# All seventeen column tiles of the side projection beside the delta-net; SiLU of every gate tile in the output stage

## The reference

```python
def rmsnorm(x, gain):
    xf = x.astype(jnp.float32)
    y = xf * lax.rsqrt(jnp.mean(xf * xf, axis=-1, keepdims=True) + RMS_EPS)
    return (y * gain.astype(jnp.float32)).astype(x.dtype)
...
    u = jnp.einsum('btd,dn->btn', rmsnorm(h, g_pre), w_in)
    sizes = (D_A, D_KV_A, D_KV_A, D_B, D_B, D_B, C_CONV, C_HEADS, C_HEADS, D_MIX)
...
def stick_breaking(q, k, v, q_pos, k_pos):
    z = jnp.einsum('bqhd,bkhd->bhqk', q, k, preferred_element_type=jnp.float32) * (HEAD_DIM ** -0.5)
    visible = k_pos[None, :] < q_pos[:, None]
    log_beta = jax.nn.log_sigmoid(z)
    log_keep = jnp.where(visible, jax.nn.log_sigmoid(-z), 0.0)
    later = lax.cumsum(log_keep, axis=3, reverse=True) - log_keep
    w = jnp.where(visible, jnp.exp(log_beta + later), 0.0)
    return jnp.einsum('bhqk,bkhd->bqhd', w.astype(v.dtype), v)
```

## Time and profile before

| | |
|---|---|
| median of 3 runs | 2087.07 us (2084.28 to 2088.69) |
| span of the profiled execution | 2087.2 us |
| PE busy | 1956.1 us, 94% of the span |
| DVE busy | 824.0 us, 39% |
| ACT busy | 759.4 us, 36% |
| POOL busy | 499.1 us, 24% |
| mean granted TensorE clock | 0.968 |
| side products (L330), of PE's time | 592.5 us in 1360 matmuls |
| HBM traffic | 51 GB/s over the span |

### The profile page before, as it was taken

One profiled execution on the slowest core, in us unless ns is written; L12 is line 12 of the kernel. 1 busy time (PEld: TensorE's weight loads), 2 busy tenths in 40 slices (PEclk: granted clock), 3 DMA queues, 4 the chain that ended last, 5 costly groups with the idle time before them and its releaser, 6 DMA issues. The chain is left out here.

```text
span 2087.2 us, 25680 instructions
## 1 busy us (share of the span) xinstructions
PE 1956.1 (94%) x9682; PEld 1222.7 (59%) x9682; DVE 824.0 (39%) x1596; ACT 759.4 (36%) x1590; POOL 499.1 (24%) x436
## 2 busy tenths in 40 slices
PE   6989993999999999999989998999999999969997
PEld 6944441666666666666645554555555555647775
DVE  5723432223222222222216775444454444553332
ACT  4413541222222222222214443344344444455564
POOL 0004312123222231223100000233332333324433
PEclk9999996999999999999998998999999999989999
DMA  4210204100000111102001112000100000165562
GB/s 127 95 32 10 65 1 27 32 27 32 21 32 27 62 57 37 32 27 67 21 28 45 41 41 73 11 21 17 61 28 11 21 7 11 39 180 155 168 191 89
DMA packets 120887, 108.13 MB, mean 52 GB/s; under 512 B 34337, under 2 KB 96065, under 8 KB 120769
## 3 DMA queue, kind: packets, MB, share of 16 engines
q1 hardware_dynamic: 117616, 95.62, 16.5%
q0 software_dynamic: 3152, 10.91, 1.4%
HBM read 65.54 MB, written 41.08 MB: 51 GB/s over the span
## 5 line engine op out<-in xcount | busy, mean ns | idle before, releaser
L330 PE MATMUL side_acc<-hT,wslot 128*128 128x512 f32 (+1 forms) x1360 | 592.5, 546 | 4.4 <-DMA wslot<-in_w_in 4.4
L1570 DVE TENSOR_TENSOR_SCAN prod<-keepb,prod 128x512 f32<-128x512 f32 (+4 forms) x184 | 208.4, 1133 | 286.8 <-ACT keepb L1509 286.4
L1552 POOL TENSOR_TENSOR beta<-beta,prod 128x512 f32<-128x512 f32 (+4 forms) x184 | 174.9, 951 | 588.0 <-DVE prod L1570 588.0
L330 PEld LDWEIGHTS side_acc<-hT,wslot 128*128 128x128 f32 x1360 | 218.3, 192 | 146.0 <-issue 135.6
L1509 ACT ACTIVATE keepb<-b_z 128x512 f32<-128x512 f32 (+4 forms) x184 | 97.7, 531 | 298.4 <-PE b_z L1443 191.2
L460 PE MATMUL acc<-hT,wslot 128*128 128x512 f32 (+1 forms) x480 | 180.6, 532 | 5.4 <-DMA wslot<-in_w_in 5.4
L1440 PE MATMUL b_z<-reg 64*128 64x512 f32 (+3 forms) x360 | 179.9, 580 | 4.8 <-PEq L1793 4.8
L724 POOL TENSOR_TENSOR atl<-at,cf 128x512 f32<-128x512 f32 x102 | 139.8, 1404 | 173.0 <-DVE at L944 173.0
L964 DVE TENSOR_TENSOR xt<-xt,b_kq 128x512 f32<-128x512 f32 x85 | 58.4, 688 | 303.5 <-PE b_kq L791 303.5
L1467 PE MATMUL b_o<-wt,vrow 128*64 128x128 f32 x1232 | 173.4, 280 | 0.5 <-DVE wt L1584 0.5
L1467 PEld LDWEIGHTS b_o<-wt,vrow 128*64 128x64 f32 x1232 | 129.5, 136 | 35.2 <-issue 33.7
(11 more groups left out here) (197 smaller groups left out, 2773.6 us busy)
## 6 DMA issues: line engine op xcount, KB each, us to landing
uT_scratch<-side_stage SPq DMA_DIRECT2D x36, 256.0 KB, 2.0
hT<-mix_scratch SPq DMA_DIRECT2D x17, 512.0 KB, 6.7
hT<-sz_scratch SPq DMA_DIRECT2D x17, 512.0 KB, 8.1
sz_scratch<-side_stage SPq DMA_DIRECT2D x32, 256.0 KB, 2.0
reg<-in_x_prompt SPq DMA_DIRECT2D x15, 512.0 KB
wslot<-in_w_in SPq DMA_DIRECT2D x15, 512.0 KB, 4.0
xres<-in_x_prompt SPq DMA_DIRECT2D x15, 512.0 KB
out_y_prompt<-yy POOLq DMA_DIRECT2D x15, 512.0 KB, 6.4
```

Of the source, the lines that this page charges most:

```text
L330: last = pe.matmul(self.acc[:, n % 2, 0:width], wslot[:, t % 2, k, :], hT[:, k, c0:c0 + width], start=(k == 0), stop=(k == KT - 1))
L1552: pool.tensor_tensor(w, w, prod[0:R, rowno[s] % 2, k0 + 1:k0 + nk + 1], ALU.mult).then_inc(w_ready, 1)
L1570: dve.tensor_tensor_scan(prod[0:R, row % 2, k0:k0 + nk][:, ::-1], kv, kv, prod[0:R, row % 2, k0 + nk:k0 + nk + 1], ALU.mult, ALU.bypass).t ...
```

## The change

`RAWZ` goes from 4 to 8, so all eight z tiles are made beside the delta-net as raw z, and `stick_breaking` gets none. `POINTS` holds 38 pieces in an iteration where it held 29 (four in all are never used: 18 x 38 = 684 for 680 pieces). In `stick_breaking` the pieces, `keep`, `gate`, the weight loads and the stores go; two tiles of its own (`kstage`, `b_kr`) take the turned keys, without the waits on the side projection; the swaps of the last two token blocks are issued at the start of the stage. In `output`, `zsig` and both SiLU instructions are twice as wide (128x1024). `SWAPS` follows from `POINTS`: units 28, 36, 50 become 28, 47, 66.

```diff
-RAWZ = 4
+RAWZ = 8
...
-                POINTS = [4, 2, 2, 2] + [2, 1, 1] + [2, 2, 1] * 3 + [0]
+                POINTS = [4, 2, 3, 2] + [3, 2, 2] + [2, 3, 2] * 2 + [2, 2, 2] + [0]
...
-                side = SideProjection(st, "silu", side_tiles)
+                kstage = sb("kstage", [P, 2, 2 * VBW], st=st)
+                b_kr = pb("b_kr", [P, 2, 512], st)
...
-                        side.transfers(sp, swap)
-
-                        sp.wait_ge(side.acc_ready, side.units)
+                        for b in range(SWAPPED, NBLK):
+                            c0, w = BLOCKS[b]
+                            sp.dma_start(mix[0:4, :, c0:c0 + w].rearrange("k p t -> p k t"), reg[:, 0:4, c0:c0 + w]).then_inc(spilled[b], 16)
+                            sp.dma_start(reg[:, KS:KS + 2, c0:c0 + w], uT[7:9, :, c0:c0 + w].rearrange("k p t -> p k t")).then_inc(qk_in[b], 16)
+                            sp.wait_ge(spilled[b], 16)
+                            sp.dma_start(reg[:, QS:QS + 2, c0:c0 + w], uT[5:7, :, c0:c0 + w].rearrange("k p t -> p k t")).then_inc(qk_in[b], 16)
...
                         for s in range(N + 4):
                             if s < N:
                                 scores(s)
-                                side.products(pe, side_piece(s), side_piece(s + 1) - side_piece(s))
...
                                 sigmoids(s)
-                                for n in side_units(s):
-                                    side.keep(act, n)
...
                                 scan(s)
-                                for n in side_units(s):
-                                    side.gate(dve, n)
```

More of the change, by code:

```diff
@@ L1293, in _, with stick_breaking @@
                         dve.tensor_copy(krow[:, :, :], b_pt[:, 0, 0:2, :]).then_inc(krow_kept, 1)
-        def stick_breaking(side_tiles):
+        def stick_breaking():
             KC = 512
@@ L1320, in stick_breaking @@
                 new = slice(SP0, SP0 + NSAMP)
[L1322 to L1327, removed]
                 steps = []
@@ L1410, in _ @@
                                 for dst, part in b_key_stores(m):
-                                    sp.dma_start(dst, side.stage[part, g % 2, (m % 2) * VBW:(m % 2 + 1) * VBW]).then_inc(krow_out[g % 2], 16)
+                                    sp.dma_start(dst, kstage[part, g % 2, (m % 2) * VBW:(m % 2 + 1) * VBW]).then_inc(krow_out[g % 2], 16)
                             for dst, src in pieces[len(pieces) * g // GROUPS:len(pieces) * (g + 1) // GROUPS]:
@@ L1471, in turn_keys @@
                         def turn_keys(g):
-                            if g < 2:
-                                pe.wait_ge(side.staged, side.units)
-                            else:
+                            if g >= 2:
                                 pe.wait_ge(krow_kept, g - 1)
@@ L1478, in turn_keys @@
                                     at = (m % 2) * VBW + a * P
-                                    last = pe.transpose(side.acc[:, g % 2, at:at + P], reg[:, KS + a, m * P:(m + 1) * P], ident)
+                                    last = pe.transpose(b_kr[:, g % 2, at:at + P], reg[:, KS + a, m * P:(m + 1) * P], ident)
                             last.then_inc(krow_turned, 1)
@@ L1519, in keep_keys @@
                             act.wait_ge(krow_turned, g + 1)
-                            if g < 2:
-                                act.wait_ge(side.stored[g], 16 * ((side.units + 1 - g) // 2))
-                            else:
+                            if g >= 2:
                                 act.wait_ge(krow_out[g % 2], krow_transfers(g % 2, g))
                             width = VBW * len(key_group(g))
-                            act.activation(side.stage[:, g % 2, 0:width], side.acc[:, g % 2, 0:width], ACT.Copy).then_inc(krow_kept, 1)
+                            act.activation(kstage[:, g % 2, 0:width], b_kr[:, g % 2, 0:width], ACT.Copy).then_inc(krow_kept, 1)
                         for s in range(N + 4):
@@ L1807, in stream_layer @@
         stage(window_attention)
-        stage(stick_breaking, z_tiles[RAWZ:])
+        stage(stick_breaking)
         mixers.close()
```

## The result

The changed kernel takes 2102.07 us (median of 5 runs, 2097.56 to 2103.44) where the kernel before takes 2088.69 in the runs beside it (5 runs, 2084.28 to 2093.01): a ratio of 1.0065, with a 95% interval from 1.0048 to 1.0081. It is slower by some 13 us, where 2081.4 us, a gain of 6, was forecast, and it lies outside the range.

A forecast was written before the change was run, and what follows sets the result against it. In the delta-net and stick-breaking, TensorE's instructions plus its gaps were taken as the bound. 118.1 - 0.9 - 123.5 - 3.9 + 1.7 + 2.7 = -5.8 us gave 2081.4 us, range 2073 to 2096.

The forecast's parts named there:

- Start of stick-breaking: Start of stick-breaking: the wait for z weights goes and cached keys are turned earlier, -3.9 us, between 0 and -6.
- first rival: Gains at the edges eaten: clock low longer at stick-breaking's start, output costs more; 2088.5 us, chance 0.26.
- A rule weighed: Skill's rule that frequent small idles make the clock swing, a danger for thinner stick-breaking steps; trace disagreed, small chance given.
- third rival: Clock falls in stick-breaking, once for each of 16 query tiles, +27 us: 2108 us, chance 0.05.
- Pieces out of stick-breaking: Stick-breaking: removing 128 wide and 32 narrow pieces makes it 123.5 us shorter if TensorE stays the bound.
- Stick-breaking without pieces: Stick-breaking: TensorE waits for VectorE's copied weights at 12 short steps behind full ones, +1.7 us.
- second rival: Stick-breaking: TensorE waits for copied weights at 52 short steps, 18.2 us in place of 1.7; 2097.9 us, chance 0.12.
- Pieces into the delta-net: Delta-net: 128 wide pieces at 0.86 us and 32 narrow at 0.25 add 118.1 us.
- Gaps of the delta-net: Delta-net: first-turn waits unchanged at 0 (-5.5 to +5); wait for normalised output shrinks, -0.9 us.
- fourth rival: Delta-net gaps fill: 5.5 us of first-turn waits and 3.5 us of smaller ones go; 2072.4 us, chance 0.07.
- Output stage: Output: wider SiLU delays the first tile +1.5 us and three loop tiles +1.2, together +2.7, between 0 and +8.
- The sum: Whole kernel: all terms added give -5.8 us, so 2081.4 us.

The follow-up runs named there:

- split1: Changed kernel with one z tile back in stick-breaking, one piece in each of its first 40 steps, 36 pieces per delta-net iteration: 2093.59 us.
- w4: Changed kernel plus four unread full-array products in step 1 of stick-breaking: 2097.39 us.
- w4col: Changed kernel plus four unread products on 128 rows and only 64 columns in step 1 of stick-breaking: 2097.25 us.
- each16: Changed kernel plus one unread full-array product behind the scores of each of the first 16 stick-breaking steps: 2107.15 us.
- w2_high: Changed kernel plus two unread full-array products at the start of stick-breaking, and `high` moved ahead of the sigmoid in output: 2073.24 us.
- a_high: Changed kernel with ScalarE's `high` of the next tile moved ahead of the sigmoid in output: 2090.44 us.
- w4half: Changed kernel plus four unread products on 64 of 128 rows, all columns, in step 1 of stick-breaking: 2117.4 us.
- zwide: Kernel before, pieces unmoved, but all eight z tiles stored raw and the wide SiLU done in output: 2096.62 us.
- w4_high: Changed kernel plus four unread full-array products at the start of stick-breaking, and `high` moved ahead of the sigmoid in output: 2076.6 us.

## Why the prediction was wrong

**What failed is "Start of stick-breaking".** It took a gain of 3.9 us and set the clock aside: "TensorE is at half clock here [...] either way; when it rises with less work is not to be read, so 0 to -6." That range assumed that the pieces had no part in the rise. They made it: with them (before, split1) or with wide work in their place (w4, w4col, each16, w2_high) the clock is up within 7 us of the first such product, and without (after, a_high) or with half-row work (w4half) it stays low for 48 us and more. In place of 0 to -6 the step should have been -3.9 + 19 in the case that happened. The first rival named the mechanism, "the clock stays low longer", but priced it at the 3.9 us that it could take back. The saving of 3.9 itself came: the cached keys were turned 3.8 us behind the first scores, at 1408.41, where before it was 8.5 us (1292.06 to 1300.52), with a piece between.

**"A rule weighed", and the third rival.** I looked at what makes the clock fall, and gave that 0.05, with a fall in each of 16 query tiles. It fell in none of them. It was low because the stage began low, after the stop of all engines between the stages, and the light work could not lift it. The right question stood in the earlier trace rows: a piece of 2.08 us says that the stage begins at half speed, and what ends that was being removed. The Trainium skill (TensorE: Matmul & The Clock Gate, "What's actually happening") says that the gate goes by how busy the engine has recently been. By it, a TensorE without a gap would be at full speed soon after the first scores; the four windows with 10.00 of 10 us busy at 0.50 do not agree, and w4half beside w4col shows that being busy doesn't tell the two cases apart.

**"Pieces out of stick-breaking" and "Stick-breaking without pieces" held.** Full steps take 2.65 us for 2.66, the waits for the copied weights came to 2.9 us (0.7 before) for the +1.7, and the stage without the low clock is as short as forecast, as w4 showed. The second rival was wrong: no row of short steps became a bound.

**"Pieces into the delta-net" and "Gaps of the delta-net".** +113.6 us for +117.2. The first turned matrix of an iteration waited 7.2 us in nine times for 5.5 in six, inside the bounds but more often than I counted; the 2.3 us for the normalised output did not shrink, so the -0.9 was wrong. The smaller waits gave back 3.5 us: for ScalarE's first copy (L891) 3.4 us before and 1.5 after, for its second (L894) 1.7 and 0.5, for the second subtraction (L964) 1.7 and 1.3. So of the fourth rival one half came, its 3.5 us, and the other, its 5.5, did not. More of the difference is the price of the pieces: TensorE's busy time in the stage grew by 114.9 us (726.05 to 840.99) for the 118.1 forecast. Behind its start each trace has one window of 25 us at 0.86 in this stage, so that does not enter the row.

**"Output stage" was under-sized.** +2.7 forecast; the row from the first product has +6.0, the start about 1 more (the first product waited 17.8 us for 16.9), and zwide put the SiLU alone at +4.1 in that row. The mechanism was the one named, the sigmoid ahead of `high` before three tiles. Sized wrongly was that only the 0.41 us of the sigmoid would be added: VectorE's split takes 2.96 us for 2.12, since it ends 1.1 us behind a GpSimd product that is twice as wide; so each wait grew by 1.1 us, and a third window went to a low clock. The bound of +8 held it. What I did not see is that the waits are needless as such: the exchange of two calls takes them all away.

**The sum**: +113.6 - 1.8 + 0.7 - 105.3 + 6.0 = +13.2. Of the 19 us between it and the forecast, about 19 are the clock in stick-breaking and 5 the output loop, less 4 in the delta-net and 1 elsewhere. The first rival came nearest in mechanism: it had the right direction for both edges and stopped at 0 where the start of the stage lost 19. The second's 2097.9 us is nearer as a number, and that is luck, since the waits it priced stayed at 2.9 us; so is the third's 2108, since no fall came.

**What stays open.** What lifted the clock in the changed kernel at last, at 1452.8, no run tells: the steps ahead of the rise are of the same kinds as those before them, only wider. w4, w4col and each16 gained less in the whole than in stick-breaking. Their output loops, and that of w4half, have four waits of up to 3.0 us where the changed kernel's profile has three:

```profile
PE b_y L1663 <- DVE mlo L1716: 11.5, 4, 3.0
```

That is 3 us of it; with `high` first, w4_high is 13.8 us faster than a_high, as it should be. Why these programs have one wait more, no run here tells. The delta-net had 864.2 and 862.7 us in w4 and w4col where the other programs with the same code there have 855.7 to 860.0. Part of that is the clock: over 352 to 382 us and 495 to 535 us it is 0.86 and 0.96 in w4, 0.92 and 0.91 in w4col, and 0.98 and 1.00 in the changed kernel. Why it is lower there is open.

## What to carry to other kernels

Before you take filler work out of a stage, look at the granted clock at its start: if the stage begins low, look for the instructions behind which it rises, and ask what would lift it without them; two to four wide products at the start made the stage 14 to 17 us shorter here (w4 beside the changed kernel, w2_high beside a_high). On an engine that works in order, put what the critical chain needs next ahead of work that waits for a transfer, and price an operation beside its neighbours as they will be after the change, not as they are.

## What the runs showed of the hardware

- TensorE without idle time stayed at a granted clock of 0.50 (1.2 GHz) for 40 us and more while it did fp32 scores on 64 rows, values on 64 columns and short turned blocks, in three kernels of three (after, a_high, w4half).
- It rose to 1.00 (2.4 GHz) within or right behind 3.56 us of full-array fp32 products (w2_high), 6.19 us of them (w4), or 4.86 us of products on 64 columns and all rows (w4col). Behind 7.19 us on 64 rows and all columns it stayed at 0.50 (w4half). Once up, it stayed up with the same light steps, over windows with 0.2 to 0.6 us idle in 10.
- The VectorE subtraction of 128x1024 took 1.22 or 1.23 us when no GpSimd product or addition was running as it began. When one was, it ended 1.08 to 1.11 us behind that one, 24 times of 24 (before and after): 2.12 us beside a product of 128x512 and 2.96 beside one of 128x1024.
